# Forgetting attention on Trainium2: the causal masks' products with fp32r operands in place of bf16 ones

## The reference, cut to what matters

```python
s = jnp.einsum('bqhd,bkhd->bhqk', q_blk, k_all, preferred_element_type=jnp.float32)
s = s + fq_blk.transpose(0, 2, 1)[..., None] - f_k[:, :, None, :]
s = jnp.where((kpos[None, :] <= qpos[:, None])[None, None], s, -jnp.inf)
p = jax.nn.softmax(s, axis=-1)
return jnp.einsum('bhqk,bkhd->bqhd', p.astype(v_all.dtype), v_all)
```

## Time and profile before

| what | value |
|---|---|
| median of 3 runs | 3189.69 us (3185.55 to 3195.04) |
| profiled execution | 3188.47 us, of which 3186.8 us are the span from its first to its last instruction |
| mean granted TensorE clock | 0.944 |
| busy over the span | PE 2895.5 us (91%), PEld 2008.2 (63%), DVE 1533.9 (48%), ACT 952.5 (30%), POOL 750.7 (24%) |
| attention phase | about 1991 to 2915 us of the span |

### The profile page before, as it was taken

The page is one execution under the profiler, slowest core; times in us unless marked ns, Lnnn a source line. Parts: engine busy times, 40 slices in busy tenths (PEclk is TensorE's granted clock), DMA queues, the critical chain, the costliest instruction groups (busy, mean ns, idle before and its releaser), DMA issues. The chain is left out here.

```text
span 3186.8 us, 43017 instructions
## 1 busy us (share of the span) xinstructions
PE 2895.5 (91%) x15730; PEld 2008.2 (63%) x15730; DVE 1533.9 (48%) x3562; ACT 952.5 (30%) x1547; POOL 750.7 (24%) x428
## 2 busy tenths in 40 slices
PE   5589999997899978999979999799999989995999
PEld 2367777776777856777757777344444444442757
DVE  1542222212877638431173125667766766763343
ACT  0322212212555544210042111144334334433000
POOL 1310000000000003000030000476767667676000
PEclk8589999998999988999989999699999999997999
DMA  9532222213565524121153221513421331303764
GB/s 340 187 87 79 54 86 80 77 47 126 178 217 189 158 95 174 73 77 48 40 178 80 73 48 53 157 35 104 114 76 51 104 92 42 107 32 124 247 199 133
DMA packets 281946, 355.41 MB, mean 112 GB/s; under 512 B 40044, under 2 KB 172460, under 8 KB 281681
## 3 DMA queue, kind: packets, MB, share of 16 engines
q1 hardware_dynamic: 279364, 344.23, 34.0%
q0 software_dynamic: 2304, 8.39, 0.7%
q10 hardware_dynamic: 72, 0.07, 0.0%
HBM read 250.28 MB, written 102.10 MB: 111 GB/s over the span
## 5 line engine op out<-in xcount | busy, mean ns | idle before, releaser
L2318 POOL TENSOR_TENSOR at_p_sum<-at_p_sum,at_p 128x1024 f32<-128x1024 f32 (+3 forms) x264 | 541.7, 2052 | 95.9 <-ACT at_p L2174 84.6
L2174 ACT ACTIVATE at_p<-psum 128x1024 f32<-128x1024 f32 (+1 forms) x320 | 286.9, 897 | 516.6 <-PE psum L2014 514.1
L2220 DVE CUSTOM_DVE_ANT_0 psum<-psum,at_f_wide 128x512 f32<-128x512 f32 (+3 forms) x640 | 376.8, 631 | 0.0
L2094 PE MATMUL psum<-at_p,at_v 128*64 128x512 f32 (+3 forms) x1280 | 305.9, 557 | 0.1
L672 POOL TENSOR_TENSOR kv_h_lo<-kv_aux,kv_h_hi 128x512 fp32r<-128x512 f32 x16 | 24.1, 1507 | 1056.8 <-ACT kv_h_hi L649 1025.9
L768 PE MATMUL psum<-kv_w_hi,kv_h_hi 128*128 128x512 f32 x512 | 201.2, 393 | 13.2 <-DVE kv_w_lo L964 13.2
L768 PE MATMUL psum<-gla_w_hi,gla_h_hi 128*128 128x512 f32 x512 | 201.3, 393 | 2.7 <-DVE gla_w_lo L964 2.7
L769 PE MATMUL psum<-kv_w_lo,kv_h_hi 128*128 128x512 f32 x512 | 200.2, 391 | 0.0
L770 PE MATMUL psum<-kv_w_hi,kv_h_lo 128*128 128x512 f32 x512 | 200.0, 391 | 0.0
L769 PE MATMUL psum<-gla_w_lo,gla_h_hi 128*128 128x512 f32 x512 | 199.5, 390 | 0.0
L770 PE MATMUL psum<-gla_w_hi,gla_h_lo 128*128 128x512 f32 x512 | 199.3, 389 | 0.0
(11 more groups left out here) (425 smaller groups left out, 6088.3 us busy)
## 6 DMA issues: line engine op xcount, KB each, us to landing
mod_w<-in_ada_w SPq DMA_DIRECT2D x12, 2048.0 KB, 18.0
at_f_wide<-F SPq DMA_DIRECT2D x32, 512.0 KB, 5.9
at_page<-in_cache_k SPq DMA_DIRECT2D x32, 512.0 KB, 3.4
gla_w_raw<-in_gla_w_in SPq DMA_DIRECT2D x6, 2048.0 KB, 8.0
mod_w<-in_kv_ada_w SPq DMA_DIRECT2D x4, 2048.0 KB, 10.0
v_gla<-gla_stage SPq DMA_DIRECT2D x32, 256.0 KB, 2.0
sg_gla<-gla_stage SPq DMA_DIRECT2D x32, 256.0 KB, 2.0
gl_sg<-sg_gla SPq DMA_DIRECT2D x16, 512.0 KB, 3.9
```

Of the source, the lines that this page charges most:

```text
L2094: mm = pe.matmul(bank_o[half[a], skip:NB], v[u][:, i, half[a]], p_tile[e % PT][:, a, skip:NB], start=(i == 0), stop=(i == R * G + R - 1), ...
L2174: act.activation(p_tile[e % PT][:, :, skip:NB], pair_of(bank_st[e % 2])[:, :, skip:NB], ACT.Exp)\
L2220: op = dve.tensor_tensor_reduce(pair_of(at(n))[:, a, 0:w], pair_of(at(n))[:, a, 0:w], f_wide[:, a, c * NB:c * NB + w], 1.0, -3.0e38, ALU.s ...
L2318: pool.tensor_tensor(p_sum[s][:, :, skip:NB], p_sum[s][:, :, skip:NB], p_tile[e % PT][:, :, skip:NB], ALU.add).then_inc(p_added, 1)
```

## The change

`attention_phase` gets three more tiles of 128x128, of type fp32r. POOL fills them at the start of the phase, ahead of its memsets, by copying `ident16`, `hide_kq` and `hide_qk`. PE waits for the three copies (semaphore `masks_made`) ahead of its first transposes. All 256 calls of `masks` then read the new tiles as weights and as moving operand. The number of products, their order, their shapes and their places are as before.

```diff
+        ident_r, hide_kq, hide_qk = (sb(n, [P, P], F32R) for n in ("ident_r", "hide_kq", "hide_qk"))
+        masks_made = sem("masks_made")
...
-                        pe.matmul(bank(bank_at + a)[:, col:col + P], g.ident16[:, :], hide[:, :], start=True, stop=False,
+                        pe.matmul(bank(bank_at + a)[:, col:col + P], ident_r[:, :], hide[:, :], start=True, stop=False,
                                   skip_group_check=True)
...
-                            masks(bank_st[e % 2], (i - R * G) * P, g.hide_kq)
+                            masks(bank_st[e % 2], (i - R * G) * P, hide_kq)
...
-                            masks(bank_max, t % R * P, g.hide_qk)
+                            masks(bank_max, t % R * P, hide_qk)
...
                 pe.sem_inc(p_used, PT)
+                pe.wait_ge(masks_made, 3)
...
-                            masks(first_max(n), a % R * P, g.hide_qk)
+                            masks(first_max(n), a % R * P, hide_qk)
...
             def _(pool):
+                for tile, src in ((ident_r, g.ident16), (hide_kq, g.hide_kq), (hide_qk, g.hide_qk)):
+                    pool.tensor_copy(tile[:, :], src[:, :]).then_inc(masks_made, 1)
                 for n, (tile, value) in enumerate(clears):
```

## The result

The changed kernel takes 3235.49 us (median of 4 runs, 3233.65 to 3246.35) against 3188.71 us before (4 runs, 3185.55 to 3195.04). The ratio is 1.0149, 95% interval 1.0131 to 1.0167, so 47.5 us more (42 to 53). The forecast was 33.5 more, its range ended at 3236; on the 3189.69 that it started from, the ratio gives 3237. The direction and the price of a call came out; the size is some 40% above the forecast, because of the clock, which the prediction left out.

A forecast was written before the change was run, and what follows sets the result against it. PE was taken to bound the attention phase; 28.7 (seven head pairs) + 3.0 (last) + 1.0 (prologue) + 0.8 (half clock elsewhere) = 33.5 us, giving 3222.0 from the profile, 3223.2 as median. Range 3211 to 3236.

The forecast's parts named there:

- PE bounds the phase, and its waits cover little: Attention head pair: PE busy 103.59 of 107.10 us, waiting 3.2 for DVE, so added PE time lengthens it nearly as much.
- Two calls per head pair were covered: Two single calls before a maximum step waiting for DVE, 0.24 and 0.67 us idle: 2 x 0.15 less per head pair.
- The pause comes from the form: Product with V to mask: 1.01 us to bf16 or another-form fp32r product, so array form, not type, makes the pause.
- faster: Rival: pauses around masks go with the type, saving 0.2 at some 200 places, 40 us, giving 3150; chance 0.04.
- hidden loads: Rival: fp32r mask loads go under the preceding product, pace stays 0.055 and time 3190; chance 0.05.
- 0.37 and 0.59 per call, 4.1 per head pair: Masks: single call 0.37 for 0.22, two in a row 0.59 for 0.33; 4.1 us more on a 107.1 head pair.
- The casts and the wait cost nothing: Start of attention: three POOL copies, estimated 1.0 us, end before PE's first transpose, which waits for DMA; cost 0.
- The prologue at 1.0: Prologue: 12 calls at half clock, DVE the busier engine, taken as 1.0 us more, range 0 to 4.9.
- Left: 4.1 us on 107.1. Seven head pairs have this pattern.: Attention steps: each of seven head pairs gets 4.1 us longer, 28.7 together; the last one gets 3.0.
- 28.7 + 3.0 + 0.8: Eight head pairs: 28.7 us for seven, 3.0 for the last, 0.8 for single calls at half clock outside the prologue.
- The guessed 0.8: Single mask calls at half clock outside the prologue: a guessed allowance of 0.8 us.
- the rival of plain fp32 speed: Rival: masks as slow as the 0.42 plain fp32 pair, +0.20 per call, 46 us in all, 3236; chance 0.07.

The follow-up runs named there:

- the two pairs of kernels whose clock doesn't fall at unit 12: Changed kernel against kernel before, both with six extra fp32r products before unit 12's wait: 3219, 3186.5; both with page work moved to units 14 and 16: 3207.5, 3173.

## Why the prediction was right, and where it was wrong

- **PE bounds the phase, and its waits cover little.** Right. Waits of the head pair at 2068 to 2180, us in total, times, longest, answering to the earlier trace rows:

```profile
PE psum L2010 <- DVE at_chunk_max L2223: 1.8, 2, 1.4
...
PE psum L2043 <- DVE at_m L2229: 0.8, 1, 0.8
...
PE psum L2016 <- DVE at_chunk_max L2223: 0.4, 1, 0.4
```
  3.0 in all after 3.2. Two calls per head pair were covered, as said: the one at 2188.11 takes 0.37 to the load behind it (2188.48), 0.36 before, and the one at 2275.33 takes 0.78 like its fellow before (2261.93 to 2262.71), with less idle time in it, 0.48 for 0.67:

```profile
2276.11 0.19 PEld L2016 LDWEIGHTS psum<-at_kT_hi,at_qT_hi 64*128 64x128 f32 x2 [0.48 <-DVE at_chunk_max L2223]
```
- **The pause comes from the form.** Right: 1.02 and 1.01. The rival "faster" is out with it, and "hidden loads" with the pace of 0.11.
- **0.37 and 0.59 per call, 4.1 per head pair.** Right: 111.28 where 111.2 was forecast, and +32.5 and +35 in the two pairs of kernels whose clock doesn't fall at unit 12, for a sum of 33.5. The reason given, that the load sets the pace, is not shown (see above).
- **The casts and the wait cost nothing.** Right: 1.0002. The casts take 0.24 each from start to start, the first memset comes 0.71 behind the first cast, `load_f` is 1.8 later, 1.1 of it by the later start of the phase, and still ends far ahead of SP's next issue; POOL, SP and PE where the attention begins, answering to the earlier trace rows:

```profile
1992.60 0.29 POOL L2299 CAST at_ident_r<-ident 128x128 fp32r<-128x128 bf16 x1 [320.75 <-POOLq L2698]
...
1993.07 0.29 POOL L2299 CAST at_hide_qk<-hide_qk 128x128 fp32r<-128x128 bf16 x1
1993.31 0.12 POOL L2303 MEMSET at_ones<- 128x32 f32 x1
...
2005.51 3.49 SPq L1919 DMA_DIRECT2D at_k_more<-f_both  x2
2015.97 0.75 SPq L1938 DMA_DIRECT2D at_q_more<-at_m_hi  x1
...
2002.38 0.72 PEld L2025 LDWEIGHTS psum<-ident,at_q_rows 128*128 128x128 f32 x4 [17.06 <-issue]
```
- **The prologue at 1.0.** Mis-sized. It was 3.3 up to the first product with V, the forecast's range being 0 to 4.9. A call there costs 0.62 instead of 0.32; 12 of them and 2 more in the first units, also at half clock, are 4.2, and over three quarters of it showed. That DVE is the busier engine of the prologue did not cover them.
- **The step that failed** is "Left: 4.1 us on 107.1. Seven head pairs have this pattern." It took the granted clock as given, because the head pair at hand stands at 1.00. After the change it falls behind the wait at unit 12, for 6.8 us in three of the four head pairs shown, and in the last head pair for 10.2 where it was 3.4. The eight head pairs grew by 43.9, against 28.7 + 3.0 + 0.8 = 32.5 forecast. The 11.4 between them: 4 x 3.0 for these falls, 1.5 for 3.4 us more at half clock at one loop's return, less 1.5 for 3.4 us fewer in the first head pair, 12.0. Filling or removing the idle time brings the difference back to 32.5 and 35. The guessed 0.8 was for calls at half clock, not for further falls. A sign was in the kernel before: in its last head pair the clock falls behind a wait of 2.08.
- **The upper end** of 3236 came from the rival of plain fp32 speed, and the result lies beside it. That is chance. Its price of 0.20 per call rested on the 0.42 of a product taken for two; the changed calls cost 0.15, and plain fp32 costs 0.43 more than bf16.

What stays open: what brings the short falls, why the clock falls in some head pairs and not in others with the same instructions, and whether it is the loads' time or another trait of the fp32r products that costs the clock. What is shown: the falls need the idle time at unit 12; where it is 1.4 us they come only in kernels with fp32r masks, and the two calls right behind it are enough; where it is 2.1 us or more they come with bf16 masks too.

## What to carry to other kernels

For a mask or any other small product with 128 weights, bf16 operands make the load 98 ns and the pace 0.055 per product, fp32r ones 189 ns and 0.11; matching the type of the neighbouring products saves no pause, since the pause belongs to the array form. A head pair read at one level of the clock prices the change only if the clock stays there: look for waits of PE near the added work, and compare with a kernel in which the wait is filled or gone; here two calls behind a wait cost 8 us beyond their price. A wait of the bounding engine that comes from another engine's side work (here the scoring of a page) is the first thing to move: 0.5% for one line.

## What the runs showed that was not expected

- The granted clock fell from 1.00 to 0.50 behind a wait of PE of 1.4 us with fp32r masks behind it, and with bf16 ones behind 2.1 us (for 3.4 us, the last head pair) and 2.4 us but not behind 1.4. Each fall of 6.8 us cost 3.0.
- A product that does nothing useful can pay: 1.5 us more of PE work per head pair made the changed kernel 0.5% faster (1.0095 against 1.0149).
- A plain fp32 product is two products with two loads; a pair of rows in the trace is then one instruction of the program.
